# Softmax weights scaled by gate over row sum on ScalarE, in place of factor blocks turned on TensorE

## The reference

```python
def masked_softmax(logits, valid, sink=None):
    ...
    e = jnp.exp(logits - m)
    den = jnp.sum(e, axis=-1, keepdims=True)
    if sink is not None:
        den = den + jnp.exp(sink - m)
    return e / jnp.where(den > 0, den, 1.0)
# then, for each branch: o = p @ v, times a sigmoid gate per token, head
# and branch (layer B only), times silu(z) per element, summed over branches
```

## Time and profile before

| | us |
|---|---|
| median of 3 runs | 1691.91 |
| lowest and highest run | 1689.2 and 1694.02 |
| the profiled execution | 1685.25 |
| its span in the profile | 1683.5 |
| TensorE busy, share of the span | 94% |
| ScalarE busy, share of the span | 36% |
| VectorE busy, share of the span | 55% |

### The profile page before, as it was taken

The page is one execution under the profiler, slowest core; times in us unless marked ns, Lnnn a source line. Parts: engine busy times, 40 slices in busy tenths (PEclk is TensorE's granted clock), DMA queues, the critical chain, the costliest instruction groups (busy, mean ns, idle before and its releaser), DMA issues.

```text
span 1683.5 us, 31856 instructions
## 1 busy us (share of the span) xinstructions
PE 1587.2 (94%) x11936; PEld 1426.0 (85%) x11936; DVE 928.0 (55%) x2398; ACT 614.2 (36%) x1356; POOL 485.1 (29%) x294
## 2 busy tenths in 40 slices
PE   4799999999799988899999999999999999997997
PEld 1688888887699987798998988989889888886897
DVE  3735544545636244565665656656466574677456
ACT  3433333343216142224434344343443434443113
POOL 1222422224911424372121211211112211158671
PEclk9799999999899989999999999999999999998999
DMA  9323233332613054310110211101010010132832
GB/s 348 141 74 113 80 115 122 111 108 89 221 51 92 13 179 125 100 38 24 42 51 23 69 46 42 76 23 42 23 40 28 23 41 23 29 104 75 268 136 101
DMA packets 82594, 145.16 MB, mean 86 GB/s; under 512 B 19170, under 2 KB 54146, under 8 KB 82274
## 3 DMA queue, kind: packets, MB, share of 16 engines
q1 hardware_dynamic: 69210, 128.64, 22.8%
q10 hardware_dynamic: 10288, 8.46, 1.6%
q0 software_dynamic: 2944, 6.04, 1.2%
HBM read 128.96 MB, written 19.35 MB: 88 GB/s over the span
## 4 chain that ended last, share of the span: by engine, by line
PE 88%; DVE 6%; issue 2%; ACT 2%; DMA 1%; SPq 1%; ACTq 0%; DVEq 0%
PE PS L1034 16%; PE PS L1036 16%; PE PS L1035 16%; PE PS L1290 11%; PE PS L1303 11%; PE PS L1270 5%; PE PS L1271 4%; PE PS L1409 2%; PE PS L1280 2%; PE PS L1232 1%; PE PS L1299 1%; DMA WR<-w_ada 1%; PE PS L1252 1%; PE PS L1385 1%; DVE MT L1809 1%
## 5 line engine op out<-in xcount | busy, mean ns | idle before, releaser
L1034 PE MATMUL PS<-HT_r,WR_r 128*128 128x344 f32 x1320 | 438.9, 333 | 4.3 <-issue 3.8
L1036 PE MATMUL PS<-HT_r,WR_r 128*128 128x344 f32 x1320 | 424.5, 322 | 0.0
L1035 PE MATMUL PS<-XT_r,WR_r 128*128 128x344 f32 x1320 | 424.0, 321 | 0.0
L676 POOL TENSOR_TENSOR WR_r<-WR,ONE 128x1024 fp32r<-128x1024 f32 x59 | 115.1, 1950 | 992.0 <-DMA WR<-w_b 598.4
L1636 ACT ACTIVATE PB<-PB,NM 128x257 f32<-128x257 f32 (+9 forms) x384 | 248.8, 650 | 163.3 <-DVE NM L2057 163.0
L1034 PEld LDWEIGHTS PS<-HT_r,WR_r 128*128 128x128 f32 x1320 | 251.4, 190 | 6.3 <-issue 5.6
L1035 PEld LDWEIGHTS PS<-XT_r,WR_r 128*128 128x128 f32 x1320 | 251.2, 190 | 0.0
L1036 PEld LDWEIGHTS PS<-HT_r,WR_r 128*128 128x128 f32 x1320 | 250.6, 190 | 0.0
L2070 DVE COPY PT<-PS 128x256 f32<-128x256 f32 (+2 forms) x192 | 121.5, 633 | 213.3 <-PE PS L1290 212.3
L1290 PE MATMUL PS<-CST,PB 128*128 128x128 f32 (+1 forms) x1360 | 227.6, 287 | 1.1 <-ACT PT L1644 1.0
L1303 PE MATMUL PS<-PT,VT 128*64 128x128 f32 x2592 | 205.1, 287 | 7.5 <-DVE SS L2110 3.4
(11 more groups left out here) (317 smaller groups left out, 2429.3 us busy)
## 6 DMA issues: line engine op xcount, KB each, us to landing
WR<-w_ada SPq DMA_DIRECT2D x64, 512.0 KB, 5.4
WR<-w_b SPq DMA_DIRECT2D x32, 512.0 KB, 3.3
WR<-w_a SPq DMA_DIRECT2D x17, 512.0 KB, 5.8
STR<-scratch SPq DMA_DIRECT2D x128, 48.0 KB, 1.8
XT<-x SPq DMA_DIRECT2D x8, 516.0 KB, 8.1
HT<-x SPq DMA_DIRECT2D x8, 516.0 KB, 7.4
HT<-x_mid SPq DMA_DIRECT2D x8, 516.0 KB, 5.1
STR<-scratch SPq DMA_DIRECT2D x128, 32.0 KB, 1.9
```

What stands on the lines that cost most here:

```text
L676: pool.tensor_tensor(high_r, raw, ONE[:, 0:1].unsqueeze(2).to_broadcast([P, NC, P]), ALU.mult).then_inc(sem("w_split"), 1)
L1034: pe.matmul(out, hw[:, k, :], high, start=(k == 0), stop=False)
L1035: pe.matmul(out, hw[:, k, :], low, start=False, stop=False)
L1036: return pe.matmul(out, lw[:, k, :], high, start=False, stop=(k == NC - 1))
```

## The change

The factor is put on the exponentials, before they are turned. There is a new step `nr` for each part:

- VectorE takes the reciprocal of the part's row sums (128x1), and in phase "b" multiplies it with the gate (128x1), into a column of NM.
- ScalarE multiplies the whole part in PB (128 rows, as many columns as keys) with this column, in place.
- For the compressed branch VectorE does all of it, with one product over 128x512.

The steps `rg`, `tr` of SS and `t1` are gone. `oe` reads the silu path itself: output times 0.5 times SZ. TensorE's wait before the turning of a unit is now for `nr` of its second part. In the list, the two `nr` steps of the unit that comes next stand behind the evictions of the unit under way: the first one behind the third group's `ev` where there are three or more groups, the other at the end of the unit, ahead of `fe` and `qc`. In phase "b" ScalarE's `nr` also waits until the `nr` before it has landed. Waits of other engines for `t1` are waits for `oe` now.

```diff
     def flush():
-        if late:
-            emit("tr", late)
-            emit("t1", late)
         for g in pending:
...
                 emit("sm", nxt["parts"][1])
-                emit("rg", ending[0])
+                emit("nr", un["parts"][0])
...
-        late = None
-        for hf in ending[0:1] if un["b"] != "cmp" else []:
-            emit("rg", hf)
         emit("tr", gs[0])
         emit("ev", gs[0])
         if nxt and not to_cmp and not early_fill:
             for x in nxt["parts"]:
                 emit("ex", x)
+        due = list(nxt["parts"]) if nxt and not to_cmp else []
         if not early_fill:
             fill(here)
...
         for a, g in enumerate(gs[1:]):
             emit("tr", g)
             emit("ev", g)
+            if a == 1 and due:
+                emit("nr", due.pop(0))
...
+        for x in due:
+            emit("nr", x)
...
+                        un = x["unit"]
+                        pe.wait_ge(sem(ph + "_nr"), un["parts"][-1]["x"] + 1)
...
+                    elif what == "nr" and x["unit"]["b"] != "cmp":
+                        un = x["unit"]
+                        sl, at = un["slot"] + x["s"], un["at"]
+                        act.wait_ge(sem(ph + "_rn"), x["r"] + 1)
+                        if ph == "b":
+                            act.wait_ge(sem("b_nr"), x["x"])
+                        p_ = PB[:, sl, at:at + un["keys"]]
+                        scale = NM[:, sl, 2:3] if ph == "a" else NM[:, sl, 3:4]
+                        act.activation(p_, p_, ACT.Copy, scale=scale).then_inc(sem(ph + "_nr"), 1)
...
+                            den = DEN[:, BR[un["b"]], s, un["qb"]:un["qb"] + 1]
+                            r = NM[:, sl, 2:3]
+                            if ph == "a":
+                                dve.reciprocal(r, den).then_inc(sem("a_rn"), 1)
+                            else:
+                                c0 = BR[un["b"]] * H + 2 * un["it"] + s
+                                step(dve.reciprocal(r, den))
+                                dve.tensor_tensor(NM[:, sl, 3:4], r, SG[:, un["qb"], c0:c0 + 1], ALU.mult).then_inc(sem("b_rn"), 1)
...
-                            dve.tensor_tensor(out, PS[:, 6, :], SS[:, :], ALU.mult).then_inc(sem(ph + "_oe"), 1)
+                            dve.scalar_tensor_tensor(out, PS[:, 6, :], 0.5, gate, ALU.mult, ALU.mult).then_inc(sem(ph + "_oe"), 1)
```

More of the change, by code:

```diff
@@ L183, in phase_plan @@
         emit("ex", x)
-    pending, late = [], None
+    if phase == "a":
+        for x in units[0]["parts"]:
+            emit("nr", x)
+    pending = []
     def flush():
-        if late:
-            emit("tr", late)
-            emit("t1", late)
         for g in pending:
@@ L259, in phase_plan @@
             emit("ex", nxt["parts"][0])
-        if un["b"] == "cmp":
-            emit("rg", ending[1])
-            late = ending[1]
-        elif ending:
-            emit("tr", ending[0])
-            emit("t1", ending[0])
         if un["b"] != "cmp" and not to_cmp:
@@ L286, in phase_plan @@
             order.append(x)
-            if x["kind"] == "p":
-                x["c"] = c
-                c += 1
+            x["c"] = c
+            c += 1
     for un in units:
         un["trs"] = max(g["n"] for g in un["groups"]) + 1
+    for r, x in enumerate(x for x in parts_ if x["unit"]["b"] != "cmp"):
+        x["r"] = r
     new = None
@@ L518, in bank_free @@
         def bank_free(ph, x):
-            if x["kind"] == "o":
-                return sem(ph + "_t1"), x["h"] + 1
             return (sem(ph + "_evd") if x["c"] % 2 else sem(ph + "_eva")), x["c"] // 2 + 1
@@ L1944, in add_mask @@
                     step(dve.tensor_tensor(m, m, CST[:, C_FAR:C_FAR + P], ALU.add))
-                def free_sums(h, it, b):
-                    if h:
-                        dve.wait_ge(sem(ph + "_oe"), h)
-                    adds = 0 if ph == "a" else len([x for x in pl["halves"] if "add" in x and x["h"] < h])
-                    if adds:
-                        dve.wait_ge(sem("b_mix"), adds)
                 if ph == "a":
@@ L2070, in pairs @@
                         dve.tensor_copy(PT[0:m, c % 2, 0:n], PS[0:m, 4 + x["n"] % 2, 0:n]).then_inc(sem(ph + "_evd"), 1)
-                    elif what == "rg":
-                        it, b, half, h = x["it"], x["b"], x["half"], x["h"]
-                        un = [u for u in pl["units"] if u["it"] == it and u["b"] == b and u["qb"] in (None, 4 * half + 3)][0]
-                        dve.wait_ge(sem(ph + "_ex"), un["parts"][-1]["x"] + 1)
-                        den = DEN[:, BR[b], :, :].rearrange("p s q -> p q s")
-                        if b == "cmp" and half == 0:
+                    elif what == "nr":
+                        un, s = x["unit"], x["s"]
+                        sl = un["slot"] + s
+                        dve.wait_ge(sem(ph + "_ex"), x["x"] + 1)
+                        if un["b"] == "cmp":
+                            c0 = 2 * un["it"]
@@ L2077, in pairs @@
                             p4 = PB[:, un["slot"], un["at"]:un["at"] + un["keys"]].rearrange("p (q s c) -> p q s c", q=QB, s=2)
+                            den = DEN[:, 0, :, :].rearrange("p s q -> p q s")
                             step(dve.tensor_reduce(den, p4, AX, ALU.add))
                             step(dve.tensor_scalar(den, den, 1.0 / BIG, None, ALU.max))
-                        rg = RG[:, :, :]
-                        step(dve.reciprocal(rg, den[:, 4 * half:4 * half + 4, :]))
-                        free_sums(h, it, b)
@@ L2083, in pairs @@
[L2083 to L2097 removed]
+                            step(dve.reciprocal(den, den))
@@ L2102, in pairs @@
                         dve.wait_ge(sem(ph + "_pv"), last["c"] + 1)
-                        dve.wait_ge(sem(ph + "_t1"), h + 1)
+                        dve.wait_ge(sem("fill_ev"), gate_done(ph, b, it, half))
+                        gate = SZ[b][:, 512 * half:512 * half + 512]
                         if b in ("a", "cmp"):
```

53 lines of the change are left out of this document (15 added, 38 removed).

## The result

The changed kernel takes 1783.21 us (median of 4 runs, 1779.65 to 1787.38) against 1692.35 us for the kernel before on the same chip. The ratio is 1.0547, with an interval of 1.0527 to 1.0567. The direction was forecast; the size was not. The forecast was +50 us with 1775 as its upper end, and it is +91 us.

What follows compares the result with a forecast made beforehand. TensorE, busy 94% of the span, was taken as the bound. Removal -27, phase "a" +19, phase "b" +40, last pair +6 and secondary waits +12 gave +50 us: 1742 against the 1692 median, range 1705 to 1775.

Steps and rivals of the forecast that it cites:

- Removal, -27 us: TensorE loses 64 groups of four transposes at 0.40 us, 25.6 us, plus 1.5 us of waits.
- VectorE's chain is covered by two projection thirds: Compressed units: reduce, reciprocal, gate and 128x512 product finish before TensorE's turning, adding 0.
- Cost of one scaling, the exponential's: Each ScalarE scaling takes as long as an exponential: 0.50 us for 256 columns, 0.82 for 640, 1.14 for 1024.
- Phase "a", +19 us: TensorE's turning waits for scalings: 4 x 0.3 + 2 x 0.6 = 2.4 us a pair, 19 us in 8 pairs.
- Phase "b", 5.0 us of exposed waits a pair: TensorE's turning waits for scalings, summed over the units of a pair; 40 us in 8 pairs.
- 0.15 for each of six more: Phase "b": 0.15 us of waiting at each of six remaining units, 0.9 us a pair.
- The product with the gate, 0.15 us each, 38 us busy, free: VectorE gains 256 small gate products, between 0.06 and 0.2 us each; its total costs nothing, having 45% to spare.
- The last pair, +6 and a pair's share, 12.5 us: The last pair has nearly no projection work as cover, so 6 us more than its ordinary share.
- Secondary waits, +12 us: Values wait for VectorE or ScalarE evictions behind scalings, output steps and small steps: 1.5 us a pair, 12 us.
- Covered and half covered: Rivals: scaling hidden, only the removal remains, 1665 us, chance 0.08; half the exposed waits hidden, 1680 to 1715, chance 0.12.
- The transposes at their durations: Rival: removed TensorE transposes are worth about 275 ns each, 70 us, sum +7, 1699 us; chance 0.02.
- The clock: Rival: gaps drop TensorE's clock to 1.2 GHz for a twentieth of the two loops, 56 us more, 1800; chance 0.04.

Runs made afterwards that it cites:

- without the scaling: Changed kernel with small reciprocals, gate product and ScalarE scaling left out for layer A, selected and window parts: 1665.61 us, 0.9877 of the kernel before.
- the table: Changed kernel with scalings placed per unit, gate product with a per-row factor, and ScalarE's wait only behind the compressed unit: 1696.27 us, 1.0033 of the kernel before.
- the run with the compressed product early: The per-unit placement version, with VectorE's compressed product moved directly behind the next unit's first score step: 1703.63 us, 1.0088 of the kernel before.
- two runs: Changed kernel with the gate product replaced by a second reciprocal (1765.12 us, 1.0444), or written with a per-row factor (1766.55 us, 1.0442).
- the last one: The per-unit placement version, with the compressed product behind both score steps but ahead of the output step: 1685.76 us, 0.9996 of the kernel before.

## Why the prediction was right about the sign and wrong about the size

**Removal, -27 us: -21.** The factor transposes were worth what their starts showed. The 6 us that are missing are a step I set at nothing: "VectorE's chain is covered by two projection thirds" did not hold. TensorE waits 6.9 us in 7 places for it without the scaling, 4.8 us after, 8.4 us with the table, and 1.3 us once the output step stands behind it; that move gave 0.37 points, 6 us, on intervals of 0.15 each way for either run. I had not added the chain up: reduce, maximum, reciprocal, product, wide product are five dependent steps, in a queue that has an output step of two more ahead.

**Cost of one scaling, the exponential's: right,** 500, 827 and 1144 ns for 0.50, 0.82 and 1.14 us.

**Phase "a", +19 us: +22,** 22.3 us of waits in 53 places. The place by place reading worked there: in the pair from 349 to 383 us the waits are 0.36 to 0.38 in four places, 0.52 and 0.65 in two and 0.15 in one, where I had four of 0.3 and two of 0.6. Each holds the 0.10 us by which TensorE starts later than I put it.

**Phase "b", 5.0 us of exposed waits a pair: 7.8.** One pair, the waits of the turning for L1632 from 1001 to 1087 us, by unit, which the width of the scalings ahead tells:

| unit `j` | forecast | measured |
|---|---|---|
| 2 | 0.8 | 0.83 |
| 8 | 0.8 | 0.90 |
| 14 | 1.2 | 1.29 |
| 10 | 0.5 | 0.30 |
| 13, 15 | 0.4 each | 0.73, 0.68 |
| 3, 4, 5, 7, 11 | 0.15 each | 0.33, 0.46, 0.49, 0.47, 0.34 |
| 12 | 0.15 | 1.00 |

The measured waits are idle times, some 0.07 us short of the delay each. The three places that were worked out from the timeline are right within 0.2 us even so (my own sum for unit 8, 1001.97 - 1001.10, was 0.87). In unit 14 the path was the one forecast: its second exponential starts 0.32 us ahead of the last turning of unit 13 before (1032.77, 1033.09) and 0.78 us behind it after (1077.13, 1076.35). The step that failed is "0.15 for each of six more": those six have 3.1 us where I put 0.9. They were set without a timeline of their own, and they are half of the places; 13 and 15, also without one, have 1.4 us where I put 0.8. Two things were left out. One is the 0.14 us from the end of a scaling to TensorE's start, where I had 0.04; the median over the 151 waits is 0.14, and 0.10 too little in each is about 15 us, worked out and not measured alone. The other is the hold. In unit 12 it is over half of the wait (GpSimd, VectorE, ScalarE, TensorE):

```profile
1062.34 2.38 POOL L670 TENSOR_TENSOR WR_r<-WR,WR_r 128x1024 fp32r<-128x1024 f32 x1
1064.04 0.70 DVE L2079 TENSOR_TENSOR NM<-NM,SG 128x1 f32<-128x1 f32 x1
...
1064.77 1.54 ACT L1632 ACTIVATE PB<-PB,NM 128x512 f32<-128x512 f32 x2 [1.02 <-DVE NM L2079]
...
1066.45 0.41 PE L1277 MATMUL PS<-CST,PB 128*128 128x128 f32 x2 [1.00 <-ACT PB L1632]
```

The product is held by 0.54 us until GpSimd ends at 1064.72; without that the wait would be 0.46, like its neighbours.

**The product with the gate, 0.15 us each, 38 us busy, free: 81 us busy, and 26 us of the time.** Its bounds of 0.06 to 0.2 us were for an instruction alone. No 128x1 product was in the trace, but a warning was, in a group I had not set beside the others. In the kernel before, 128x512 with both inputs in SBUF:

```profile
L2114 DVE TENSOR_TENSOR MT<-MT,SS 128x512 f32<-128x512 f32 x32 | 26.2, 818 | 1.1
```

The same elements with one input in PSUM take 685 ns. In the run with the compressed product early this group has a mean of 720, so most of the difference is not the instruction but whom it meets. This term is 17 us of hold and 9 us of plain length. It was in no rival. Without the hold the time would be some 1766 us, inside the range, though still 24 us above the forecast.

**The last pair, +6 and a pair's share, 12.5 us: 24.** "No cover there" was right, the size not. From 1592 to 1626 us GpSimd is busy for 33.3 of 34 us, and all ten products are held. The two of one unit, ahead of TensorE's longest wait (3.49 us, to 1598.21):

```profile
1592.67 1.90 DVE L2079 TENSOR_TENSOR NM<-NM,SG 128x1 f32<-128x1 f32 x1
...
1594.68 2.31 DVE L2079 TENSOR_TENSOR NM<-NM,SG 128x1 f32<-128x1 f32 x1
```

With the second reciprocal in its place this stretch (last compressed values to the end) is 198.4 instead of 211.8 us.

**Secondary waits, +12 us: smaller.** In the seven pairs from 740 to 1570 us values wait 7.8 us in 14 places for VectorE's evictions and output steps, and without the scaling in none; I had 10.5 us for seven pairs. This term ran the other way. With the delay of some 109 us at the turning it about makes up the 117 us.

**In sum,** in profiled executions: 1685.25 to 1783.1 is +98 us where the sum had +50 (the medians differ by 91, since the execution of before lay 6.7 us under its median). Of the 48 between, 6 are the removal. The scaling's terms were 77 us and are 117: of these 40, 17 are the hold, about 15 the slower restart, and some 8 are left, small places and the product's own length, less what the secondary waits had too much. The 17 were isolated by two runs, and the 6 by the last one; the other two are read from rows.

**The rivals.** Covered and half covered: not in the change, but a list with other places reaches 0.9996, so most of the scaling can be covered, some 97 of 117 us. "A row that leaves no choice" was too strong: it left none with the scalings where the change put them. The transposes at their durations: no, 21 us. The upper end of 1775 took 33 us for the long scaling; 0.09 us for each of two scalings in 150 places gives 27, and the rest has no source. The clock: over the attention loop of phase "b" its mean is 1.00 to two places (window, us, TensorE busy, granted clock, DMA share, GB/s; before, then after):

```profile
740.00:1490.00 750.00, 747.87 (x5963) 1.00 0.13 37
```

```profile
740.00:1570.00 830.00, 756.96 (x5923) 1.00 0.13 34
```

After, with TensorE 91% busy, this mean hides one fall. The longest gap of the loop ends at 771.91, and from about 773.1 to 776.5 us the clock is at its 1.2 GHz level (the gap, then the same columns):

```profile
771.91 0.63 PE L1277 MATMUL PS<-CST,PB 128*128 128x128 f32 x4 [2.27 <-ACT PB L1632]
```

```profile
773.00:777.00 4.00, 4.00 (x18) 0.57 0.03 6
```

Behind the other 84 waits for the scaling, the next longest 1.73 us, TensorE stayed at 2.4 GHz. The rule of the Trainium skill on frequent micro-idles, cited in the prediction, does not show in that loop: the many short gaps brought no fall, and one fall followed the longest. A fall of 3.4 us costs at most 1.7. In the last pair, with gaps of up to 3.5 us and much less work in between, the clock fell more often (after, same columns):

```profile
1592.00:1604.00 12.00, 7.76 (x56) 0.80 0.52 145
1604.00:1616.00 12.00, 9.18 (x94) 0.92 0.32 93
1616.00:1628.00 12.00, 4.86 (x27) 0.65 0.20 57
```

This rival's mechanism is there for some 36 us at a mean of 0.79. The kernel before has such falls in its last pair too (0.86 over 1510 to 1560 us, which is 14 us at the lower level; after it is 0.78 over 1595 to 1665, 31 us). Of the last pair's 24 us, 18.8 are waits for the scaling in 13 places; what the clock's share is was not separated by a run.

## What to carry to other kernels

Where an engine at 94% gives work away to an engine that is half idle, cost the new chain at every place where the full engine meets it, not at the worst three: the many small waits decided here. A step of one element a row is not free if it has two SBUF inputs and GpSimd is at work. Written with a per-row factor operand it cost 54 ns more here and was not held once in 256; look at the longest of such a group all the same, since a step of 16 columns with a constant was held. When a step has to be slipped into in-order queues, look at each queue for what waits behind it: the same compressed product was worth +0.5, +0.7 (the same within the noise) or -0.4 points against the table's version in three places a few steps apart.

## What the runs showed of the hardware that I had not expected

- A VectorE product of two 128x1 SBUF inputs took 0.16 us alone and up to 2.37 us when a GpSimd product of 128x1024 had started 0.05 us before it. At 128x1, with one input (reciprocal, 165 ns at most) or a factor operand (212 to 217 ns in 256 cases), it was not held.
- One SBUF input was no protection at 128x16: a VectorE minimum with a constant took 0.18 us three times and 1.07 to 1.86 us five times in the kernel before, each of the five ending 0.03 us behind a GpSimd instruction.
- How often that happens depends on where the step stands: the mean was 317 ns in the change's places, 464 ns in the earlier ones.
- TensorE's first turning began 0.14 us after the end of the ScalarE instruction it waited for (268.96 to 269.10, and at the median of 151 waits).
- The hold also falls on VectorE's 128x16 product of two inputs in the compressed chain: 2.16 us from 952.92 in the run with that chain early, against 0.19 us alone.
- TensorE's granted clock fell once in 830 us with 85 waits for the scaling: to its lower level for some 3.4 us, 1.2 us behind the longest gap, 2.27 us. Behind a gap of 1.73 us (to 1181.1) it did not. In the run with the compressed product early it fell five times in 740 us, three times right behind gaps of 2.0 to 2.1 us; around a gap of 3.47 us in the last pair it was 0.65 over 12 us.
